# Which engine makes the low parts of eight expert tiles while the experts are selected

## The reference, cut to what matters

```python
def chunk_fn(hc):
    q = (hc @ w_query).reshape(TOKEN_CHUNK, PEER_HEADS, 2, PEER_HALF)
    sc = jnp.einsum('thpd,pnd->thpn', q, sub_keys).astype(jnp.float32)
    vals, idx = lax.top_k(sc, PEER_TOPK)
    cand = vals[:, :, 0, :, None] + vals[:, :, 1, None, :]
    cand_idx = idx[:, :, 0, :, None] * N_KEYS + idx[:, :, 1, None, :]
    ...
    top_s, pos = lax.top_k(cand, PEER_TOPK)
    expert_idx = jnp.take_along_axis(cand_idx, pos, axis=-1)
    gate = jax.nn.softmax(top_s, axis=-1)
    u = expert_u[expert_idx]
    act = jax.nn.gelu(jnp.einsum('thkd,td->thk', u, hc).astype(jnp.float32), approximate=False)
    vv = expert_v[expert_idx]
    return jnp.einsum('thk,thkd->td', (gate * act).astype(hc.dtype), vv)
```

## Time and profile before

| | us |
|---|---|
| median of 3 runs | 2364.92 (2364.58 to 2365.05) |
| the profiled execution, whole | 2365.04 |
| its span in the profile | 2363.2 |
| TensorE busy | 2309.6 (98%) |
| VectorE busy | 1715.6 (73%) |
| GpSimd busy | 1019.4 (43%) |
| ScalarE busy | 872.1 (37%) |

### The profile page before, as it was taken

The page is one execution under the profiler, slowest core; times in us unless marked ns, Lnnn a source line. Parts: engine busy times, 40 slices in busy tenths (PEclk is TensorE's granted clock), DMA queues, the critical chain, the costliest instruction groups (busy, mean ns, idle before and its releaser), DMA issues.

```text
span 2363.2 us, 34880 instructions
## 1 busy us (share of the span) xinstructions
PE 2309.6 (98%) x12272; PEld 1980.0 (84%) x12272; DVE 1715.6 (73%) x3188; ACT 872.1 (37%) x1386; POOL 1019.4 (43%) x1080
## 2 busy tenths in 40 slices
PE   7999999999999999999998899999999999999998
PEld 5885788888888887678898898888899999999998
DVE  5467743332389986867999898588787778888886
ACT  3137222222232243832434455444433333333333
POOL 4530555656655556155541001344455433444440
PEclk9999999999999999999999999999999999999999
DMA  5320223333323323122232467999999989999993
GB/s 170 97 64 28 72 89 98 98 98 105 102 96 98 98 89 112 42 72 84 90 100 88 172 256 265 297 370 320 323 336 333 326 298 315 327 346 332 329 350 126
DMA packets 213107, 437.69 MB, mean 185 GB/s; under 512 B 111760, under 2 KB 116368, under 8 KB 209936
## 3 DMA queue, kind: packets, MB, share of 16 engines
q1 hardware_dynamic: 65376, 235.44, 29.8%
q0 software_dynamic: 39440, 142.10, 16.7%
q10 hardware_dynamic: 108192, 58.92, 8.6%
HBM read 401.81 MB, written 30.41 MB: 183 GB/s over the span
## 4 chain that ended last, share of the span: by engine, by line
PE 75%; DVE 15%; issue 4%; POOL 4%; ACT 1%; DMA 1%; DVEq 0%; POOLq 0%; ACTq 0%; SPq 0%
PE bank L2370 21%; PE bank L1831 16%; PE bank L1833 16%; PE bank L1832 16%; POOL lo L656 3%; DVE ohg L1731 2%; PE bank L1989 1%; DVE lo L1670 1%; PE bank L2000 1%; PE bank L1976 1%; DVE oh L1727 1%; DVE oh L1728 1%; PE bank L2311 1%; DVE idx L1629 1%; DVE scb L1622 1%
## 5 line engine op out<-in xcount | busy, mean ns | idle before, releaser
L656 POOL TENSOR_TENSOR lo<-raw,hi 128x256 fp32r<-128x256 f32 (+1 forms) x740 | 631.4, 885 | 772.2 <-ACT hi L775 553.8
L1831 PE MATMUL bank<-inH,hi 128*128 128x512 f32 (+1 forms) x2112 | 778.1, 368 | 30.0 <-DVE inL L1198 14.7
L1833 PE MATMUL bank<-inH,lo 128*128 128x512 f32 (+1 forms) x2112 | 769.5, 364 | 0.0
L1832 PE MATMUL bank<-inL,hi 128*128 128x512 f32 (+1 forms) x2112 | 769.1, 364 | 0.0
L1831 PEld LDWEIGHTS bank<-inH,hi 128*128 128x128 f32 x2112 | 398.5, 189 | 82.0 <-issue 16.8
L1832 PEld LDWEIGHTS bank<-inL,hi 128*128 128x128 f32 x2112 | 398.9, 189 | 45.0 <-issue 0.2
L1833 PEld LDWEIGHTS bank<-inH,lo 128*128 128x128 f32 x2112 | 398.4, 189 | 42.7
L775 ACT ACTIVATE hi<-raw 128x1024 fp32r<-128x1024 f32 x236 | 248.0, 1056 | 403.9 <-PE bank L1833 389.7
L1146 ACT ACTIVATE hi<-raw 128x1024 fp32r<-128x1024 f32 x204 | 215.6, 1057 | 197.9 <-PE bank L2370 197.8
L711 POOL DMA_INDIRECT rows<-rows_u,expert x128 | 188.9, 1476 | 188.1 <-DVE dots L1773 167.1
L1764 DVE TENSOR_TENSOR lo<-raw,hi 128x1024 fp32r<-128x1024 f32 x208 | 253.3, 1219 | 19.8 <-ACT hi L1146 18.6
(11 more groups left out here) (331 smaller groups left out, 2759.7 us busy)
## 6 DMA issues: line engine op xcount, KB each, us to landing
raw<-stream SPq DMA_DIRECT2D x440, 512.0 KB
Gd<-gates ACTq DMA_DIRECT2D x32, 768.0 KB
gates<-stage_a ACTq DMA_DIRECT2D x12, 1024.0 KB, 4.5
gates<-stage_b ACTq DMA_DIRECT2D x12, 1024.0 KB, 4.3
tbl<-gqa ACTq DMA_DIRECT2D x8, 384.0 KB, 3.3
A<-spilled POOLq DMA_DIRECT2D x8, 384.0 KB
xT<-x SPq DMA_DIRECT2D x4, 512.0 KB, 9.0
h_rep<-h_tok POOLq DMA_DIRECT2D x16, 128.0 KB
```

The lines of the kernel that those rows point to most:

```text
L656: ins = pool.tensor_tensor(lo[:, r, part], raw[:, r, part], hi[:, r, part].bitcast(F32), ALU.subtract)
L1831: pe.matmul(bank, wh, xh, start=start, stop=False)
L1832: pe.matmul(bank, wh, xl, start=False, stop=False)
L1833: return pe.matmul(bank, wl, xh, start=False, stop=stop_)
```

## The change: tiles 12 to 19 go to GpSimd

`POOLED` goes from 12 to 20. GpSimd's loop over expert tiles runs to tile 19, and VectorE's eight low parts between the steps of the selection go. VectorE starts again at tile 20, as before.

```diff
-POOLED = 12
+POOLED = 20
...
                     chain(dve.tensor_reduce(sel[:, t % 2, 1 + s, :].rearrange("p (m j) -> p m j", j=2),
                                             eq[:, :, 0:TOPK // 4, :].rearrange("p m a j -> p m j a"), axis=AX_X, op=ALU.add))
-                    low(S_PEER + POOLED + 2 * t + s)
                 dve.wait_ge(gexp, t + 1)
...
-            u = POOLED + 2 * TT
+            u = POOLED
             for n in range(NB):
                 onehots(n)
```

## The result

| | before | after |
|---|---|---|
| median of 7 runs each, on one chip | 2367.42 us | 2373.9 us (2371.15 to 2376.47) |
| ratio of the runs, 95% interval | | 1.0031 [1.0021, 1.0040] |
| the profiled execution, whole | 2365.04 us | 2373.56 us |
| its span | 2363.2 us | 2371.7 us |

The change makes the kernel slower, by 7.3 us going by the ratio (0.31%, 5.0 to 9.5 us); the two medians stand 6.5 us apart. The forecast was +6.1 us and 2371.1; the time is 2373.9, inside the range but 2.8 us above the number. The kernel before took 2367.42 here, 2.5 us more than in the three runs on which the sum was put.

A forecast was written before the change was run, and what follows sets the result against it. VectorE's selection chain ahead of tile 20's low part was taken as the bound. Blocking by GpSimd adds 15.2 us, removed low parts save 9.1: +6.1 on 2365.0 gives 2371.1 us, range 2367 to 2374.5.

The forecast's parts named there:

- The bound: VectorE's time through the selection, 1243 to 1300.9, delays tile 20's low part; after 1320 TensorE is full.
- What is taken away, 9.1 us: Eight low parts leave VectorE's selection chain, two per block, at 1.14 us each.
- rival 1: Engines don't block each other outside tiles 10 and 11: VectorE's chain 9.1 us shorter, total 2355.9; chance 0.06.
- What is added, 15.2 us: GpSimd's low parts of tiles 12 to 19 block VectorE in the selection: six times 2.08 us, two times 1.37.
- tile 18's turn: GpSimd's low part of tile 18 follows 17's, comes beside a reduction, and holds VectorE for 1.4 us.
- The base: Time before the change on which the sum was put: 2365.0 us, from a profiled 2365.04 and median 2364.92.
- the turns: GpSimd and VectorE alternate on memory in the selection; spread from two beside reductions and 2.0 to 2.2 us per turn.
- Whatever tile 20 is moved by, the end is moved by: After 1320 TensorE is full, so tile 20's delay, +6.1 us, passes unchanged to the kernel's end.
- I count no new loss from the clock: At tile 20 TensorE's gap grows from 6.5 to 11 us, yet slow starts add nothing beyond those before.

The follow-up runs named there:

- half of the change: GpSimd makes the low parts of tiles 12 to 15, VectorE those of 16 to 19, against the kernel before: 2369.92 us, ratio 1.0013.
- the pieces: The changed kernel, but GpSimd makes each low part of tiles 12 to 19 in four 256-column instructions: 2369.25 us, ratio 1.0014 to the kernel before.

## Why the prediction came out as it did

**The bound.** Right. TensorE passed the 160 us behind tile 20 unchanged, and the first gate product moved with the selection.

**What is taken away, 9.1 us.** Right as work: the low parts are gone from VectorE. As a gain by itself it would have been 6.6, not 9.1; the step that gave rival 1 its size left out ScalarE's exponential, which the forecast called ready in each block. It is ready only while low parts or the blocking delay VectorE. The forecast's own sum did not hang on it.

**What is added, 15.2 us.** Right, place by place. Measured from the start of the selection the divisions came at 22.70, 39.48 and 63.79 us for blocks 0, 1 and 3, and the forecast's were at 22.8, 39.2 and 63.5 (from 1243.07; its 1265.9 is a start, its 1282.6 and 1306.9 are ends). The sum is +6.25 where +6.1 was said. Mis-sized in the second trace: tile 18's turn, which I put at 1.37 beside a reduction, was 2.1, for +6.99. A term that hangs on where an arrival falls within a few tenths should have carried both values in the number of its spread, not only in the words.

**TensorE.** `turn(1)` waited 5.62 (about 6 said), `turn(2)` 2.02 (3), tile 20 10.06 (11). `turn(3)` waited 2.23 us for the last division, a wait that cost nothing beyond the same gap. Tile 20 at 1317.15 against 1317.7, of which 0.67 is the earlier start of the selection. L1712 started at 1311.41 (near 1312 said). Tile 19's high part started at 1285.31 (1286.2 said).

**GpSimd.** Wrong in detail: I said 3.3 us for its low parts. Those that came singly took 2.4 to 2.7, tiles 17 and 18 5.45 together, and only the first four come near it, with 12.03 together. In the rows a low part waits for VectorE's instruction in progress (tile 14's starts at 1256.76, 0.4 us before L1688 ends, and takes 2.67), and then VectorE's next one waits for it.

**The base.** This step failed, and it is the larger part of the miss. The sum was put on 2365.0, from a median of 2364.92 over three runs. Later medians of the same kernel were 2367.42 (the one that the result stands beside), 2366.51, 2366.45 and 2367.01, with single runs from 2362.2 to 2373.9. So 2.4 of the 2.8 us by which the number is low are in the base; 2367.4 + 6.1 would have given 2373.5. The range of 2368 to 2374 for the sum took its spread from the turns alone and had none for the base.

**"Whatever tile 20 is moved by, the end is moved by", and "I count no new loss from the clock".** This step failed too, in the traces. It was true at tile 16 and tile 20, of which it spoke. But the chain has a second place, some 210 us later, where TensorE stops because VectorE stands before a gathered row, and the forecast put it at nothing without looking at it: the row was in the trace of before (2.82 us). In after it was 3.99 and 3.30 us and the clock fell behind it, and the tails were 2.8 and 3.2 us longer in the two traces. The term should have been 0 to 3.5, not 0. What it is worth in the median isn't shown. Against the kernel before of the same runs the forecast was +6.1 and the measurement +7.3 by the ratio (5.0 to 9.5) and +6.5 by the medians, with 6.4 to 7.1 of it ahead of the first gate product.

The executions of one kernel differ by several us, and the two traces of before (2365.04 and 2364.85) lie at the low side of its runs. A sum put on one such trace leaves out what other executions add.

**What stays open.** Whether the change as such makes the stop longer. Its two traces have 3.99 and 3.30 us against 2.82 and 2.67, but half of the change has 3.14 and the pieces 2.50. The row's transfer alone took 11.54 and 10.75 us in the two traces of before, 12.45 and 12.21 in those of after, 11.87 with half of the change and 13.72 with the pieces, where it was issued 2.2 us sooner; no run separates what makes it longer. The ratio of 7.3 us with 6.4 to 7.1 in the chain leaves up to 0.9 us for it, less than the measurement can tell. And with 3.06 us followed by a clock of 0.91 and 3.14 by 1.00, the length of a stop alone doesn't decide what comes behind it. What makes the rest of the scatter is open too.

## What to carry to other kernels

Before a two-input operation is moved from VectorE to GpSimd, look for a place where the two already overlap and read what VectorE loses there: here 2.1 us for an operation that costs VectorE 1.14 itself, so the engine with idle time was the dearer one. Instead of the engine change the place: the one low part for which TensorE stood longest, made ahead of the copies on VectorE, gave 6 us, and with tiles 16 to 19 one place earlier and the gathered row's use moved back it was 10.7 to 12.3 (2354.76, ratio 0.9955). Follow a shift to the end of the program: a later stop of TensorE that waits for a transfer can take back or add some us. And take the base of a sum from more than three runs, when single runs of the kernel lie 10 us apart.

## What the runs showed of the hardware

- GpSimd in 1024-column instructions holds a two-input VectorE instruction by 2.1 us, in 256-column pieces by 0.41 us, one piece for each VectorE instruction. It holds the small ones too: the division of 0.29 us took 2.51.
- The loss is uneven: a single low part on GpSimd took at most 2.67 us instead of 2.37, and four in a row 12.03 instead of 9.48, while a VectorE instruction of 1.22 us took 3.31.
- A reduction isn't held: 0.69 us beside GpSimd and without it.
- Behind stops of 2.50 to 2.82 us, and behind one of 3.14, the granted clock of the next 20 us was 1.00, that is 2.4 GHz throughout. Behind stops of 3.06, 3.30, 3.77 and 3.99 us it was 0.91 or 0.92, and behind one of 4.43 us 0.85, so a part of the 20 us ran at 1.2 GHz.
- A table load on ScalarE took 1.28 us; with it ahead of the exponential VectorE stood 2.42 us once the low parts were gone.
- The transfer of the first gathered row took 10.8 to 14.0 us in the ten traces of the table, with the same instruction.
